# Transposes put singly between matmul passes, in a projection by products of seven and in the retention heads, with the gating of a head ahead of its statistics

## What is computed

```python
h = rmsnorm(x, g_norm)
u_p, z_p, q, k, v, z_r, gates = split(h @ w_in)
y_pool = (pool(u_p) @ w_pool_group * pool_scale * silu(z_p)) @ w_branch_pool
# per head (4 heads, q and k 256 wide, v 512 wide), chunk by chunk, with a decaying state s
o = (q k^T * decay) v + q_dec s ;  s = gamma^C s + k_dec^T v
o = (o - mean(o)) * rsqrt(var(o) + eps) * gn_ret
y_ret = (o * silu(z_r)) @ w_branch_ret
out = rmsnorm(x + (sigmoid(g_p) * y_pool + sigmoid(g_r) * y_ret) @ w_out, g_final)
```

## Time and profile before

| what | value |
|---|---|
| median of 3 runs | 2873.5 us (2870.02 to 3494.84) |
| the profiled execution | 2872.27 us |
| its span, first to last instruction | 2870.5 us |
| TensorE matmuls busy | 2809.4 us, 98% of the span |
| VectorE, ScalarE, GpSimd busy | 1814.7, 1124.9, 677.9 us |
| mean granted TensorE clock | 0.995 |
| phase A, phase B | to about 1700 us, and from there |

### The profile page before, as it was taken

One profiled execution on the slowest core, in us unless ns is written; L12 is line 12 of the kernel. 1 busy time (PEld: TensorE's weight loads), 2 busy tenths in 40 slices (PEclk: granted clock), 3 DMA queues, 4 the chain that ended last, 5 costly groups with the idle time before them and its releaser, 6 DMA issues.

```text
span 2870.5 us, 36707 instructions
## 1 busy us (share of the span) xinstructions
PE 2809.4 (98%) x13504; PEld 2256.7 (79%) x13504; DVE 1814.7 (63%) x2581; ACT 1124.9 (39%) x1900; POOL 677.9 (24%) x454
## 2 busy tenths in 40 slices
PE   6999999999999999999999999999999999999998
PEld 5888888888877777777777777877887788778875
DVE  7657566667555365555666656775677567756774
ACT  5444444444554443443434433433333333333331
POOL 4343433435332233434343320000000000000000
PEclk9999999999999999999999999999999999999999
DMA  4544544444564344453534456577448744884496
GB/s 136 190 153 143 182 147 154 155 176 152 173 229 140 114 149 163 159 182 121 186 138 154 159 233 246 171 278 310 183 169 278 310 186 167 277 314 186 166 335 242
DMA packets 281881, 552.80 MB, mean 193 GB/s; under 512 B 24217, under 2 KB 166937, under 8 KB 270560
## 3 DMA queue, kind: packets, MB, share of 16 engines
q1 hardware_dynamic: 281447, 550.18, 54.1%
q0 software_dynamic: 160, 0.19, 0.0%
q10 hardware_dynamic: 96, 0.07, 0.0%
HBM read 375.59 MB, written 175.14 MB: 192 GB/s over the span
## 4 chain that ended last, share of the span: by engine, by line
PE 89%; DVE 4%; issue 3%; DMA 2%; ACT 1%; POOL 1%; SPq 0%; ACTq 0%; DVEq 0%; POOLq 0%
PE bank L1315 28%; PE bank L1317 27%; PE bank L1316 27%; PE bank L1365 1%; PE bank L1388 1%; DMA raw<-in_w_branch_ret 1%; PE bank L1502 1%; DVE wa_lo L2139 1%; PE bank L1616 1%; DVE xa_lo L2139 0%; PE bank L1604 0%; PE bank L1594 0%; DVE xs L2153 0%; DVE c_out L2139 0%; PE bank L1310 0%
## 5 line engine op out<-in xcount | busy, mean ns | idle before, releaser
L1315 PE MATMUL bank<-xa_hi,wa_hi 128*128 128x512 f32 x2240 | 890.0, 397 | 3.8 <-ACT part_s L1842 3.1
L1316 PE MATMUL bank<-xa_lo,wa_hi 128*128 128x512 f32 x2240 | 874.9, 391 | 0.0
L1317 PE MATMUL bank<-xa_hi,wa_lo 128*128 128x512 f32 x2240 | 874.8, 391 | 0.0
L1315 PEld LDWEIGHTS bank<-xa_hi,wa_hi 128*128 128x128 f32 x2240 | 421.4, 188 | 106.0 <-issue 21.5
L1317 PEld LDWEIGHTS bank<-xa_hi,wa_lo 128*128 128x128 f32 x2240 | 421.0, 188 | 90.0
L1316 PEld LDWEIGHTS bank<-xa_lo,wa_hi 128*128 128x128 f32 x2240 | 421.6, 188 | 82.8
L2139 DVE TENSOR_TENSOR wa_lo<-w_raw,wa_hi 128x512 fp32r<-128x512 f32 x320 | 310.8, 973 | 190.1 <-ACT wa_hi L1835 189.0
L2139 DVE TENSOR_TENSOR wa_lo<-w_sum,wa_hi 128x512 fp32r<-128x512 f32 x240 | 193.9, 808 | 275.4 <-ACT wa_hi L1835 275.4
L2139 DVE TENSOR_TENSOR w_lo<-raw,w_hi 128x512 fp32r<-128x512 f32 (+1 forms) x288 | 181.8, 658 | 196.6 <-ACT w_hi L1949 196.5
L1835 ACT ACTIVATE wa_hi<-w_raw 128x512 fp32r<-128x512 f32 x320 | 200.9, 628 | 245.4 <-PE bank L1317 241.7
L1949 ACT ACTIVATE w_hi<-raw 128x512 fp32r<-128x512 f32 (+1 forms) x288 | 166.7, 603 | 313.4 <-PE bank L1317 224.6
(11 more groups left out here) (249 smaller groups left out, 4334.7 us busy)
## 6 DMA issues: line engine op xcount, KB each, us to landing
w_raw<-in_w_in SPq DMA_DIRECT2D x80, 1024.0 KB, 5.4
v_d<-turned SPq DMA_DIRECT2D x64, 512.0 KB, 3.2
qk_s<-qk_d SPq DMA_DIRECT2D x32, 1024.0 KB, 7.7
v_s<-v_d SPq DMA_DIRECT2D x32, 1024.0 KB, 11.4
raw<-in_w_branch_ret SPq DMA_DIRECT2D x128, 256.0 KB, 4.6
tabs<-in_c_rope SPq DMA_DIRECT2D x16, 1024.0 KB, 6.9
qk_d<-high SPq DMA_DIRECT2D x32, 512.0 KB, 4.3
qk_d<-c_low SPq DMA_DIRECT2D x32, 512.0 KB, 5.2
```

The source lines that it names most:

```text
L1315: pe.matmul(out, lh, rh, start=first, stop=False, skip_group_check=onto)
L1316: pe.matmul(out, lh, rl, start=False, stop=False, skip_group_check=onto)
L1317: return pe.matmul(out, ll, rh, start=False, stop=last, skip_group_check=onto)
```

## The change

In phase A `turn` and `x_transposes` are taken apart: one transpose goes behind each of the four `split_product` calls of a product (after 3, 6, 9 and 12 passes). `turn` quarter q moves from behind product q + 1 into product q + 2. An x place stays at its product but lies inside it, and its waits stand before its first transpose, after the third pass. Where two places share a product, both put a transpose behind each call.

In phase B the 16 transposes of head hb - 1 go singly before the passes of `update(hb, 0)` and `output(hb, 0)`, from the sixth pass on (`turn_og(hb - 1, 5, 0)`). Those of head 3 go before the 12 passes of `group(b, 0)`, two before each of the first four and then one each (`turn_og(hb, 0, 4)`). The waits of `turn_og` stand before its first transpose. On VectorE `gate_og(hb - 1)` comes ahead of `statistics(hb, 0)`. The program has the same instructions otherwise.

```diff
@@ -1303,17 +1304,28 @@
...
+            def x_transpose(n, i, bank, k):
+                if k == 0:
+                    x_operand_ready(pe, n, i)
+                w = slice(k * P, (k + 1) * P)
+                mm = pe.transpose(banks[bank][:, w], x_operand(n, i)[:, w], ident[:])
+                if k == KH - 1:
+                    mm.then_inc(x_turned, 1)
+
             def x_transposes(n, i, bank):
-                x_operand_ready(pe, n, i)
-                src = x_operand(n, i)
                 for k in range(KH):
-                    mm = pe.transpose(banks[bank][:, k * P:(k + 1) * P], src[:, k * P:(k + 1) * P], ident[:])
-                mm.then_inc(x_turned, 1)
-
-            def split_product(out, lh, ll, rh, rl, first, last, onto=False):
-
+                    x_transpose(n, i, bank, k)
+
+            def split_product(out, lh, ll, rh, rl, first, last, onto=False, ahead=None):
+
+                if ahead:
+                    ahead()
                 pe.matmul(out, lh, rh, start=first, stop=False, skip_group_check=onto)
+                if ahead:
+                    ahead()
                 pe.matmul(out, lh, rl, start=False, stop=False, skip_group_check=onto)
+                if ahead:
+                    ahead()
                 return pe.matmul(out, ll, rh, start=False, stop=last, skip_group_check=onto)
@@ -1340,15 +1352,44 @@
...
                 s = n % SLOTS
+                turning = j and kind(j - 1) in ("k", "v") and 2 <= i < 6
                 for k in range(KH):
...
                                        xa_lo[:, i, k, :], first and k == 0, k == KH - 1, not first)
-                mm.then_inc(product, 1)
-
-            def turn(j, q):
+                    if k == KH - 1:
+                        mm.then_inc(product, 1)
+                    if turning:
+                        turn(j - 1, i - 2, k)
+                    beside_x(j, i, k)
+
+            def beside_x(j, i, k):
+
+                for place in range(PROD):
+                    n = step(j, i, 5 + SPREAD[place])
+                    if n is not None:
+                        m = PROD * (n - PAIRS) + place
+                        if k == 0 and m < 2:
+                            pe.wait_ge(turn_lo, 4 * before(NJ, "k", "v"))
+                            pe.wait_ge(r_step, r_x_done)
+                        elif k == 0:
+                            pe.wait_ge(x_copied, m - 1)
+                        x_transpose(n, BESIDE[place], 6 + m % 2, k)
+
+            def turn(j, q, k):
...
                 n = 4 * before(j, "k", "v") + q
+                i, e = k // 2, k % 2
+                tile = 2 * (q % 2) + i
+                if k == 0:
+                    turn_ready(j, q, t, n)
+                mm = pe.transpose(banks[6 + q % 2][:, (2 * i + e) * P:(2 * i + e + 1) * P],
+                                  c_out[:, j % 2, t, e, tile * P:(tile + 1) * P], ident[:])
+                if k == 3:
+                    mm.then_inc(turn_mm, 1)
+
+            def turn_ready(j, q, t, n):
+
                 if kind(j) == "k":
@@ -1359,12 +1400,6 @@
...
                     rides_copied(pe, j + 2)
-                for i in range(2):
-                    tile = 2 * (q % 2) + i
-                    for e in range(2):
-                        mm = pe.transpose(banks[6 + q % 2][:, (2 * i + e) * P:(2 * i + e + 1) * P],
-                                          c_out[:, j % 2, t, e, tile * P:(tile + 1) * P], ident[:])
-                mm.then_inc(turn_mm, 1)
@@ -1400,30 +1435,19 @@
...
                         one_product(j, i)
-                    if j and kind(j - 1) in ("k", "v") and 1 <= i < 5:
-                        turn(j - 1, i - 1)
-                    for k in range(PROD):
-                        n = step(j, i, 5 + SPREAD[k])
-                        if n is not None:
-                            m = PROD * (n - PAIRS) + k
-                            if m < 2:
-                                pe.wait_ge(turn_lo, 4 * before(NJ, "k", "v"))
-                                pe.wait_ge(r_step, r_x_done)
-                            else:
-                                pe.wait_ge(x_copied, m - 1)
-                            x_transposes(n, BESIDE[k], 6 + m % 2)
                     if j == SAMPLE_JOB + 2 and i == 0:
-            def columns_unit(u, outs, rh, rl, first, last, done):
+            def columns_unit(u, outs, rh, rl, first, last, done, ahead=None):
                 pe.wait_ge(w_lo_done, u + 1)
...
                     w = slice(c * P, (c + 1) * P)
-                    mm = split_product(banks[out][:, :], w_hi[:, s, w], w_lo[:, s, w], rh, rl, first, last)
+                    mm = split_product(banks[out][:, :], w_hi[:, s, w], w_lo[:, s, w], rh, rl, first, last,
+                                       ahead=ahead)
                     if last:
@@ -1447,7 +1471,7 @@
...
-            def update(hb, c):
+            def update(hb, c, ahead=None):
                 s = hb % 2
@@ -1458,10 +1482,10 @@
...
                         mm = split_product(banks[6 + d][:, :], kt_s[s][:, c, 0, j, w], kt_s[s][:, c, 1, j, w],
-                                           v_s[s][:, c, 0, j, :], v_s[s][:, c, 1, j, :], j == 0, j == 1)
+                                           v_s[s][:, c, 0, j, :], v_s[s][:, c, 1, j, :], j == 0, j == 1, ahead=ahead)
                     mm.then_inc(up_mm, 1)
-            def output(hb, c):
+            def output(hb, c, ahead=None):
                 s, b, h = hb % 2, hb // HEADS, hb % HEADS
@@ -1484,23 +1508,40 @@
...
                             split_product(out, qk_s[s][:, 0, 0, d, q], qk_s[s][:, 0, 1, d, q],
-                                          st_hi[:, d, :], st_lo[:, d, :], d == 0, False)
+                                          st_hi[:, d, :], st_lo[:, d, :], d == 0, False, ahead=ahead)
                     for j in range(t + 1):
...
                         mm = split_product(out, sc_hi[:, c, k], sc_lo[:, c, k], v_s[s][:, c, 0, j, :],
-                                           v_s[s][:, c, 1, j, :], not cross and j == 0, j == t)
+                                           v_s[s][:, c, 1, j, :], not cross and j == 0, j == t, ahead=ahead)
                     mm.then_inc(o_mm, 1)
-            def turn_og(hb):
-                if hb:
-                    pe.wait_ge(y_added, KT * hb)
-                if hb % HEADS == 0 and hb:
-                    pe.wait_ge(out_squared, KT * (hb // HEADS))
-                pe.wait_ge(normed, 4 * hb + 4)
-                for vt in range(4):
-                    for i in range(NT):
-                        mm = pe.transpose(banks[2 + vt][:, i * P:(i + 1) * P], og[:, i, vt * P:(vt + 1) * P], ident[:])
+            def turn_og_tile(hb, n):
+                if n == 0:
+                    if hb:
+                        pe.wait_ge(y_added, KT * hb)
+                    if hb % HEADS == 0 and hb:
+                        pe.wait_ge(out_squared, KT * (hb // HEADS))
+                    pe.wait_ge(normed, 4 * hb + 4)
+                vt, i = n // NT, n % NT
+                mm = pe.transpose(banks[2 + vt][:, i * P:(i + 1) * P], og[:, i, vt * P:(vt + 1) * P], ident[:])
+                if i == NT - 1:
                     mm.then_inc(ogt_mm, 1)
+
+            def turn_og(hb, first, double):
+
+                passes = itertools.count(-first)
+
+                def ahead():
+                    n = next(passes)
+                    if n < double:
+                        some = range(2 * n, 2 * n + 2) if n >= 0 else ()
+                    else:
+                        some = range(n + double, n + double + 1)
+                    for k in some:
+                        if k < 4 * NT:
+                            turn_og_tile(hb, k)
+
+                return ahead
@@ -1515,7 +1556,7 @@
...
-            def group(b, g):
+            def group(b, g, ahead=None):
                 n = GROUPS * b + g
@@ -1527,7 +1568,7 @@
...
                     columns_unit(b * UB + MIX[g] + kt, outs, pl_hi[:, g % 2, kt, :], pl_lo[g // 2][:, g % 2, kt, :],
-                                 kt == 0, kt == 1, mix_mm)
+                                 kt == 0, kt == 1, mix_mm, ahead)
@@ -1720,10 +1761,9 @@
...
                     hb = b * HEADS + h
-                    update(hb, 0)
-                    output(hb, 0)
-                    if h:
-                        turn_og(hb - 1)
+                    ahead = turn_og(hb - 1, 5, 0) if h else None
+                    update(hb, 0, ahead)
+                    output(hb, 0, ahead)
                     update(hb, 1)
@@ -1733,8 +1773,7 @@
...
                 hb = b * HEADS + HEADS - 1
-                group(b, 0)
-                turn_og(hb)
+                group(b, 0, turn_og(hb, 0, 4))
                 group(b, 1)
@@ -2674,9 +2713,9 @@
...
                     new_state(hb, 0)
-                    statistics(hb, 0)
                     if h:
                         gate_og(hb - 1)
+                    statistics(hb, 0)
                     if b and h == 0:
...
```

(1 more changed line is left out.)

## The result

The changed kernel takes 2921.6 us (median of 6 runs, 2919.4 to 2922.7) against 2873.5 for the kernel before: ratio 1.0168 with a 95% interval of 1.0157 to 1.0179, so 48 us slower. The profiled execution has a span of 2920.2 us, 49.7 more than the 2870.5 of before. The forecast of 2931 was 9 us too high, inside its range.

What follows compares the result with a forecast made beforehand. TensorE, with matmuls in flight for 98% of the span, was taken as the bound. 7.7 - 5.4 + 15.5 + 5.8 + 2.1 + 17.0 + 1 + 4.6 + 5.1 + 5.6 = +59.0 on 2872.3 gave 2931 us, range 2900 to 2948.

Steps and rivals of the forecast that it cites:

- Singles don't hide: All 752 moved transposes: a single one between passes costs 0.122 us, 0.109 plus 0.013, and saves nothing.
- crossings: Stepping between passes and single transposes, all moved places: 0.013 us per extra crossing, together +7.7 us (0 to +15).
- The rival on the other side: All 752 transposes: singles hide between passes, 2882 us at 0.057 us each, 2854 at 0.02; chance 0.09.
- `turn` later: Phase A, k and v transposes 3 passes later: 8 waits of 0.68 us just covered, -5.4 us.
- x copies: Phase A, x places: waits for bank copies inside the product, 3.4 us in one row group, +15.5 for four.
- x operands: Phase A, x transposes wanting normalised x earlier: 1.8, 2.0 and twice 1 us over the row groups, +5.8 us.
- The last x place: Phase A's last x place, copy hanging on the ring's DMA: wait grows from 2.7 to 4.8 us, +2.1 us.
- Head 1: Phase B, head 1's transposes wait for normalised tiles: 5.65 us in each of blocks 1 to 3, +17.0 us.
- y: Phase B, heads 2 and 3: transposes wait for the additions to y, 0.75 us six times, +4.6 us.
- Groups: Phase B, `group(b, 0)`: transposes wait for y with no pass in between, 1.27 us four times, +5.1 us.
- Gating first: VectorE, `gate_og` ahead of `statistics`: costs nothing on the path, nor does it bring time.
- The clock: Behind waits of 5.65, 4.0 and 4.8 us: granted clock falls, 1.1 us each, +5.6 us (0 to 8.5).

Runs made afterwards that it cites:

- `heads_only`: Kernel before with only the heads' and pooling groups' single transposes and the gating ahead of the statistics; projection as before: 2903.8 us, ratio 1.0112.
- `turn_only`: Kernel before with only the projection's k and v transposes put singly, quarter q inside product q + 2: 2869.9 us, ratio 0.9988.
- `turn_later`: Kernel before with k and v transposes still in blocks of 4, each block one product later: 2869.8 us, ratio 0.9983.
- `covered`: Kernel before with k and v blocks one product later, and only heads 2 and 3 transposed singly with gating ahead for them: 2865.8 us, ratio 0.9964.
- the last experiment: Kernel before with k and v transposes replaced by plain 64-column matmuls with full loads, eight singly in a product: 2907.6 us.
- `x_late`: Changed kernel with a place's x transposes two behind the third and two behind the fourth quarter of their product: 2905.8 us, ratio 1.0108.

## Why the prediction was right, and where it was off

- **Singles don't hide**: right, 0.1215 us against the 0.122 priced. But the crossings were over-priced. Their 0.013 was read as an extra on 0.109; a block of 4 costs 0.118 each, so `turn` pays 2.0 us more, not 3.7. In the heads the 16 singles cost 0.2 us in `update` and `output` and give 0.34 back behind. Only in x does the price hold, some 0.35 us for a group's 28. Together about 2 us of the 7.7. The rival on the other side has nothing for it in any trace: no single short matmul here costs under 0.11 us. The Trainium skill's 56 ns ("TensorE: Matmul & The Clock Gate", "Back-to-back issue gap"), which that section gives for an isolated gap, is seen in none of them.
- **`turn` later**: right, the eight waits are gone. With 2.0 us for the singles that is -5.4 + 2.0 = -3.4, and -3.5 was measured.
- **x copies**: the waits of the first group are 0.30, 1.39, 0.78 and 0.29 us, with 0.16 each for the modelled end 3.4, the sum foretold. Over the groups 14.2 against 15.5.
- **x operands**: 1.74, 1.02, 2.0 more in the third and 0.54, with 0.16 where a wait is new: 5.8 us, as foretold.
- **The last x place** failed: 4.8 us were foretold and 1.39 measured, 1.1 less than before in place of 2.1 more. The step was that a copy which hangs on the ring's DMA keeps its time while TensorE comes earlier. With the waits ahead of it the DMA was no longer late. ScalarE's copies at this place, before and after:

```profile
825.95 1.33 ACT L1792 ACTIVATE x_out<-bank 128x512 f32<-128x512 f32 x2 [3.74 <-DMA x_d<-x_out]
843.10 1.07 ACT L1831 ACTIVATE x_out<-bank 128x512 f32<-128x512 f32 x2
```

Of the waits that the sum had, this is the one where they overlapped. In block 0 the new wait took the place of an old one, as foretold.
- **Head 1**: 5.55 us in blocks 1 to 3 against 5.65, and 3.98 in block 0 against 4. **y**: 0.59 us six times (0.75 with the modelled end, as foretold). **Groups**: 1.30 us against 1.27; with the modelled end 1.46, which the prediction left out.
- **Gating first** was the worst step in its reasoning though the number came out. "It costs nothing" was right against the kernel before. "Nor does it bring time" compared it with before, where the block of transposes (1.9 us) still lay between `output` and `branch`, and not with the change without it: 23 us.
- **The clock** was under-sized. Three long waits of head 1 cost 1.3, 2.6 and 1.9 us over their length, the 3.80 us one of x 2.8, that of block 0 about 0.5 more than the one it replaced: about 9 us against 5.6. The earlier trace rows were read as 3.4 us at the lower level behind a wait of 2.5. With one twice as long it is 6.8 or, in block 2, about 10, and only what falls into the wait itself is free. Nor does it hold that a wait of 2.7 us costs no clock. It did not in the profile of the earlier trace rows; but `heads_only` runs the same phase A as the kernel before, and its profile has the same last x wait and then (0.09 + 0.25) x 5 / 0.5 = 3.4 us at the lower level, for 1.5 us more (timeline, then windows):

```profile
824.79 1.11 PE L1311 MATMUL bank<-ident,xq 128*128 128x128 f32 x4 [2.80 <-ACT x_out L1831]
...
820.00:825.00 5.00, 2.20 (x10) 1.52 (x9) 0.25 (x1) 0.89 (x3) 0.00 (x0) 0.91 0.89 284
825.00:830.00 5.00, 5.00 (x20) 4.17 (x20) 1.18 (x2) 2.43 (x5) 1.29 (x1) 0.75 0.56 161
```

The profiles of `turn_only`, `turn_later` and `covered` have it there too. So whether such a wait costs clock differs between executions, and a figure of a us or two for one place is not the change's alone.

Between the 59.0 us foretold and the 49.7 between the traces lie 9.3. The crossings were 5.5 too high, the last x place 3.2, the x copies 1.3, and block 0 about 1: its wait took the place of old waits almost whole. Another 2.1 lie in the clock at the start, which nobody foretold and which is not the change's. The other way went the clock behind the waits, 3.5 too low, and the groups, 0.8. So the mechanism of waits was right, and that the sum came within 9 us is in part luck: crossings and clock were wrong in opposite directions.

## What to carry to other kernels

Where TensorE is in flight for 98% of the time, moving short work earlier gains nothing unless its operand and its bank are ready there: read, for each new place, when the operand is written and when the bank is copied, and put it behind the later one. Moving it later (`turn`) is free as long as somebody has slack behind. An edit on another engine has to be priced with and without the rest of the change, since it can be the cover that the rest needs.

## What the runs showed of the hardware that was not expected

- A lone matmul of 64 streamed columns between passes costs 0.118 us, one of 128 columns 0.1215, and those of a block of 4 0.118 each. In the blocks of eight on 64 rows, with loads still 128 columns wide, they follow each other in 0.062 us, so a load of 128 columns isn't always 0.11. The Trainium skill ("TensorE: Matmul & The Clock Gate", section "LDWEIGHTS") has columns / 1.2 ns for every load, whatever the rows, 107 ns here: the loads of the last experiment (0.11 apart) agree, those on 64 rows don't.
- Going from passes on 128 rows to a transpose on 64 and back costs 0.40 us, against 0.118 without the change of rows. The Trainium skill ("TensorEngine Tiling (Array Packing)", section "Key Properties") says that changing the tiling mode drains TensorE; the 0.32 and 0.20 us steps fit that, though no trace shows that it is a drain.
- Such a chopped stream also lost clock: mean 0.941 over that kernel, against 0.995 before and 0.998 with the same work in blocks (one run each).
- The same program gets the lower clock at a place in one execution and not in another: behind a wait of 2.7 us of phase A in four traces but not in that of the kernel before, and in the first product in the traces of the kernel before and of `x_late` alone. Each costs 1.5 to 2.1 us.
